# Weight sums of a seven-product FFN stage: GpSimd-issued accumulating transfers in place of VectorE adds, and token sums on VectorE in place of GpSimd

## The reference

```python
D_FF = 2816
def swiglu(h, wi, wo):
    gu = h @ wi
    return (jax.nn.silu(gu[..., :D_FF]) * gu[..., D_FF:]) @ wo

h = rmsnorm(x, ng[4]) * (1.0 + m(7)) + m(6)
x = x + 0.5 * m(8) * rmsnorm(swiglu(h, lw['ffn_wi'][1], lw['ffn_wo'][1]), ng[5])
```

## Time and profile before

| | |
|---|---|
| median of 3 runs | 3124.38 us (3122.71 to 3128.81) |
| the profiled execution's own time | 3123.3 us |
| its span | 3121.5 us |
| PE busy | 2986.2 us, 96% of the span |
| DVE, ACT, POOL busy | 1967.7, 1128.4, 448.3 us |
| TensorE clock granted, mean | 0.974 of full speed |

### The profile page before, as it was taken

The page is one execution under the profiler, slowest core; times in us unless marked ns, Lnnn a source line. Parts: engine busy times, 40 slices in busy tenths (PEclk is TensorE's granted clock), DMA queues, the critical chain, the costliest instruction groups (busy, mean ns, idle before and its releaser), DMA issues.

```text
span 3121.5 us, 63011 instructions
## 1 busy us (share of the span) xinstructions
PE 2986.2 (96%) x26544; PEld 2675.1 (86%) x26544; DVE 1967.7 (63%) x2951; ACT 1128.4 (36%) x1757; POOL 448.3 (14%) x475
## 2 busy tenths in 40 slices
PE   7999999999988899999999999999999889899998
PEld 5999978996777699998789998789877777899986
DVE  3677556556766766765657675652566767688735
ACT  3111245235543441113531112542454435344334
POOL 1000101002323220001100001110022423500100
PEclk8999999999899999999999999999998989999999
DMA  5344344310000234443444333432010004022235
GB/s 225 135 161 153 123 128 162 125 41 27 29 5 13 104 112 158 161 148 111 140 142 161 145 131 130 143 125 84 28 50 7 3 13 149 36 95 82 82 122 168
DMA packets 62655, 324.35 MB, mean 104 GB/s; under 512 B 8753, under 2 KB 12401, under 8 KB 42993
## 3 DMA queue, kind: packets, MB, share of 16 engines
q1 hardware_dynamic: 62448, 321.39, 29.4%
HBM read 318.05 MB, written 3.31 MB: 103 GB/s over the span
## 4 chain that ended last, share of the span: by engine, by line
PE 82%; DVE 8%; DMA 4%; ACT 3%; issue 3%; POOL 0%; SPq 0%; DVEq 0%; ACTq 0%; POOLq 0%
PE PS L2565 39%; PE PS L2677 16%; PE PS L2632 7%; DMA wo<-in_wo 3%; PE PS L2575 3%; PE PS L787 2%; PE PS L1559 2%; DVE wo_lo L3068 2%; PE PS L811 1%; ACT wo_hi L2796 1%; PE PS L1538 1%; PE PS L734 1%; PE PS L1551 1%; PE PS L799 1%; PE PS L1482 1%
## 5 line engine op out<-in xcount | busy, mean ns | idle before, releaser
L2565 PE MATMUL PS<-h_hi,wi_hi 128*128 128x384 f32 (+1 forms) x2784 | 668.3, 310 | 10.5 <-issue 10.5
L2565 PE MATMUL PS<-h_lo,wi_hi 128*128 128x384 f32 (+1 forms) x2784 | 666.1, 309 | 0.0
L2565 PE MATMUL PS<-h_hi,wi_lo 128*128 128x384 f32 (+1 forms) x2784 | 666.0, 309 | 0.0
L2565 PEld LDWEIGHTS PS<-h_hi,wi_hi 128*128 128x128 f32 x2784 | 438.3, 188 | 13.6 <-issue 12.9
L2565 PEld LDWEIGHTS PS<-h_lo,wi_hi 128*128 128x128 f32 x2784 | 438.4, 188 | 0.7
L2565 PEld LDWEIGHTS PS<-h_hi,wi_lo 128*128 128x128 f32 x2784 | 438.2, 188 | 0.7
L3068 DVE TENSOR_TENSOR wo_lo<-wo,wo_hi 128x1024 fp32r<-128x1024 f32 x208 | 256.2, 1232 | 256.4 <-ACT wo_hi L2796 255.3
L2677 PE MATMUL PS<-wo_hi,a_hi 128*128 128x512 f32 x968 | 393.4, 406 | 20.9 <-DVE wo_lo L3068 12.8
L2677 PE MATMUL PS<-wo_hi,a_lo 128*128 128x512 f32 x968 | 378.3, 391 | 0.0
L2677 PE MATMUL PS<-wo_lo,a_hi 128*128 128x512 f32 x968 | 378.1, 391 | 0.0
L2388 DVE SCALAR_TENSOR_TENSOR macc<-wm,csil,macc 128x512 f32<-128x512 f32 x448 | 337.0, 752 | 15.9
(11 more groups left out here) (367 smaller groups left out, 4932.0 us busy)
## 6 DMA issues: line engine op xcount, KB each, us to landing
wi<-in_wi SPq DMA_DIRECT2D x88, 1024.0 KB, 5.0
wo<-in_wo SPq DMA_DIRECT2D x176, 512.0 KB, 3.6
wm<-in_wm SPq DMA_DIRECT2D x36, 2048.0 KB, 7.7
wi<-in_win SPq DMA_DIRECT2D x24, 1024.0 KB, 5.3
wo<-in_wout SPq DMA_DIRECT2D x32, 512.0 KB, 3.6
wq<-in_wq SPq DMA_DIRECT2D x2, 1024.0 KB, 5.0
out_y_sample<-x SPq DMA_DIRECT2D x4, 512.0 KB, 6.7
lvl<-in_lvl SPq DMA_DIRECT2D x2, 896.0 KB, 6.2
```

Source lines behind the costliest of these rows:

```text
L2565: mm = pe.matmul(PSF[0:cols, at:at + GW[g]], st, h[:, k, GA[g]:GA[g] + GW[g]], start=(k == 0 and q == 0), stop=(k == KD - 1 and q == 2))
```

## The change

The seven products are chosen differently, so that each weight sum is the one before it plus one more block of the weights as they lie in HBM. The sums are then made by transfers that POOL issues with an add: `weights_added` adds a 128 x 4 x 128 block (256 KB, rows of 512 bytes) from HBM to a block of the loaded `wi`. There are four a unit: one on the up block (semaphore `s_tu`) and three, one after the other, on the gate block `raw(j, 0, 0)` (`s_ts`). The three change the same block, which is operand 0, then 1, then 2, then 6. So each must wait until the operand before it is cut, and each cut must wait until the transfer has landed. DVE's weight sums are gone. The token sums are made by DVE in place of POOL, two of them before the multiplications of unit 0, two between units 1 and 2. Parts 2, 3, 4 and 6 are accumulated on PSUM banks that already hold parts 0, 1 and 2, after ACT has copied the intermediate value out (`part_copy`). A fast unit uses three banks in place of four, and three DVE additions in place of five; the signs are put right in the final multiplications. The cuts are in another order, `PART_ORDER` = 0, 3, 1, 4, 5, 2, and part 6 of a unit is cut during that unit itself.

```diff
 FAST = {5: 4}
 HT = TOK // 2
 HK = KD // 2
-FAST_BANK = (0, 1, 2, 3, 0, 2, 3)
-CUT_ORDER = (0, 2, 3, 1, 4, 5, 6)
+FAST_BANK = (0, 1, 0, 1, 0, 2, 0)
+SUM_END = (3, 5, 10, 12)
+LOW_END = (6, 7, 13, 14)
+PART_ORDER = (0, 3, 1, 4, 5, 2)
 
...
@@ -359,7 +361,7 @@
 
         def part_source(i, j):
 
-            return (raw(j, 0, 0), raw(j, 0, 0), t3[:], raw(j, 0, 1), raw(j, 1, 0), t4[:], raw(j, 1, 1))[i]
+            return raw(j, *((0, 0), (0, 0), (0, 0), (1, 1), (0, 1), (1, 0), (0, 0))[i])
 
         def part_free(eng, n, u, i):
...
@@ -2462,7 +2464,7 @@
                 if V >= 2:
                     sp.wait_ge(s_wol, V - 1)
                 if b == 0 and n in FAST:
-                    sp.wait_ge(s_pd, 6 * (w0(n) + NF - 1 - FAST[n]) + 2)
+                    sp.wait_ge(s_pd, last_part(n, 2))
                 sp.dma_start(wo[:, V % 2, :, :].rearrange("p k n -> p (k n)"),
                              src[b % 2][OUT_ORDER[SUBS[s]][(b // 2) % OUT_UNITS[SUBS[s]]]]).then_inc(s_wo[V % 2], 16)
@@ -2608,28 +2610,27 @@
                 w, U0 = w0(n) + u - FAST[n], FAST[n]
                 for i in range(7):
                     if i < 6:
-                        pe.wait_ge(s_pl, 6 * w + cut_position(i) + 1)
+                        pe.wait_ge(s_pl, 6 * w + PART_ORDER.index(i) + 1)
                     else:
                         pe.wait_ge(s_wil, u0(n) + u + 1)
-                    if u < U0 + 2:
-                        if i < 4:
-                            pe.wait_ge(s_eb, u0(n) + U0 - (1 if u == U0 and i < 3 else 0))
+                    if i == 0 and u < U0 + 2:
+                        pe.wait_ge(s_eb, u0(n) + u - 1)
                     elif i == 0:
-                        pe.wait_ge(s_pa, 2 * (w - 2) + 2)
-                    elif i < 4:
-                        pe.wait_ge(s_pv, 5 * (w - 2) + (1, 4, 5)[i - 1])
-                    if i == 4:
-                        pe.wait_ge(s_pa, 2 * w + 1)
-                    if i in (5, 6):
-                        pe.wait_ge(s_pv, 5 * w + i - 3)
-                    if u == U0 and i in (1, 2, 3, 6):
-                        pe.wait_ge(s_sl, 4 * list(FAST).index(n) + {3: 1, 1: 2, 2: 3, 6: 4}[i])
-                    dst = PS[:, 4 * (u % 2) + FAST_BANK[i], 0:HT]
+                        pe.wait_ge(s_ea, u0(n) + u - 1)
+                    if i in (1, 5) and u >= U0 + 2:
+                        pe.wait_ge(s_pv, 4 * (w - 2) + (1 if i == 1 else 3))
+                    if i in (2, 3, 4):
+                        pe.wait_ge(s_pa, 4 * w + i - 1)
+                    if i == 6:
+                        pe.wait_ge(s_pv, 4 * w + 2)
+                    if u == U0 and i in (1, 2, 3, 4):
+                        pe.wait_ge(s_sf, LOW_END[-1] * fast_before(n) + LOW_END[(0, 1, 3, 2)[i - 1]])
+                    dst = PS[:, 3 * (u % 2) + FAST_BANK[i], 0:HT]
                     for k in range(HK):
                         a_hi_, a_lo_ = moving(i, k)
                         w_hi_, w_lo_ = part_hi[i][:, k, :], part_lo[i][:, k, :]
                         for q, (st, mv) in enumerate(((w_hi_, a_hi_), (w_hi_, a_lo_), (w_lo_, a_hi_))):
-                            mm = pe.matmul(dst, st, mv, start=(i < 4 and k == 0 and q == 0), stop=True,
+                            mm = pe.matmul(dst, st, mv, start=(i in (0, 1, 5) and k == 0 and q == 0), stop=True,
                                            skip_group_check=True)
                     mm.then_inc(s_pd if i < 6 else s_in, 1)
@@ -2823,15 +2824,15 @@
                 j, w = u % 2, w0(n) + u - FAST[n]
                 act_.wait_ge(s_wi[j], 16 * (u0(n) // 2 + 1) + 8 * (u - j))
                 part_free(act_, n, u, i)
-                if i in (2, 3):
-                    act_.wait_ge(s_ts, 4 * w + (1 if i == 2 else 2))
-                if i in (1, 5):
-                    act_.wait_ge(s_ts, 4 * w + (3 if i == 1 else 4))
+                if i in (1, 2, 6):
+                    act_.wait_ge(s_ts, 16 * (3 * w + {1: 1, 2: 2, 6: 3}[i]))
+                if i == 4:
+                    act_.wait_ge(s_tu, 16 * (w + 1))
                 act_.activation(part_hi[i][:], part_source(i, j), ACT.Copy).then_inc(s_ph if i < 6 else s_wih, 1)
 
             def sum_high(n, m):
 
-                act_.wait_ge(s_sf, 10 * list(FAST).index(n) + (3, 5, 8, 10)[m - 1])
+                act_.wait_ge(s_sf, LOW_END[-1] * fast_before(n) + SUM_END[m - 1])
...
+            def fast_scalar(n):
...
+                    part_copy(n, u, 0, f_p1, 0)
                     if not last:
-                        for i in (0, 2, 3, 1):
+                        part_high(n, u + 1, 0)
+                    part_copy(n, u, 1, f_p5, 1)
+                    part_copy(n, u, 2, f_u2, 0)
+                    part_high(n, u, 6)
                     if last:
...
                     else:
-                        for i in (5, 6):
+                        for i in (3, 1, 4, 5):
                             part_high(n, u + 1, i)
+                    act_.wait_ge(s_pv, 4 * w + 3)
+                    act_.activation(f_p1[:], f_p1[:], ACT.Silu).then_inc(s_pa, 1)
+                    act_.wait_ge(s_in, u0(n) + u + 1)
+                    act_.wait_ge(s_eb, u0(n) + u)
+                    act_.activation(f_s2[:], PS[:, 3 * (u % 2), 0:HT], ACT.Silu).then_inc(s_ea, 1)
+                    if not last:
+                        part_high(n, u + 1, 2)
...
             def cut_wo(n, b):
                 V = V0(n) + b
                 dve.wait_ge(s_woh, V + 1)
+                if b == 1 and n in FAST:
+                    dve.wait_ge(s_pd, last_part(n, 4))
                 dve.tensor_tensor(wo_lo[:, V % 2, :, :], wo[:, V % 2, :, :], wo_hi[:, V % 2, :, :].bitcast(F32),
                                   ALU.subtract).then_inc(s_wol, 1)
 
...
+            def sum_of(n, m):
+
+                a, b = sums[(m - 1) % 2][:], sums[m % 2][:]
...
+                if m == 1:
+                    dve.tensor_tensor(a, hi_(1, 1), hi_(1, 0), ALU.subtract).then_inc(s_sf, 1)
+                    dve.wait_ge(s_sf, base_ + 1)
+                    dve.tensor_tensor(a, a, lo_(1, 1), ALU.add).then_inc(s_sf, 1)
+                    dve.wait_ge(s_sf, base_ + 2)
+                    dve.tensor_tensor(a, a, lo_(1, 0), ALU.subtract).then_inc(s_sf, 1)
+                elif m == 3:
+                    dve.tensor_tensor(a, hi_(0, 0), hi_(1, 0), ALU.subtract).then_inc(s_sf, 1)
+                    dve.wait_ge(s_sf, base_ + 1)
+                    dve.tensor_tensor(a, a, lo_(0, 0), ALU.add).then_inc(s_sf, 1)
+                    dve.wait_ge(s_sf, base_ + 2)
+                    dve.tensor_tensor(a, a, lo_(1, 0), ALU.subtract).then_inc(s_sf, 1)
+                else:
+                    c = m // 2 - 1
+                    dve.scalar_tensor_tensor(out=a, in0=b if m == 2 else a, scalar=-1.0, in1=hi_(0, c), op0=ALU.mult,
+                                             op1=ALU.subtract).then_inc(s_sf, 1)
+                    dve.wait_ge(s_sf, base_ + 1)
+                    dve.tensor_tensor(a, a, lo_(0, c), ALU.subtract).then_inc(s_sf, 1)
+
...
             def fast_vector(n):
...
+                sum_low(n, 1)
+                sum_low(n, 2)
+                sum_of(n, 3)
+                sum_of(n, 4)
+                hidden(n, U0 - 2, 0)
...
+                    bank = lambda b: PS[:, 3 * (u % 2) + b, 0:HT]
                     if not last:
                         part_low(n, u + 1, 0)
+                    dve.wait_ge(s_pd, 6 * w + 4)
+                    dve.wait_ge(s_pa, 4 * w + 3)
+                    dve.tensor_tensor(f_u2[:], f_u2[:], bank(1), ALU.add).then_inc(s_pv, 1)
+                    part_low(n, u, 6)
...
+                        part_low(n, u + 1, 3)
+                        part_low(n, u + 1, 1)
+                    dve.wait_ge(s_pd, 6 * w + 5)
+                    dve.tensor_tensor(f_p5[:], f_p5[:], bank(0), ALU.add).then_inc(s_pv, 1)
...
+                        part_low(n, u + 1, 4)
+                    dve.wait_ge(s_pd, 6 * w + 6)
+                    dve.tensor_tensor(f_p1[:], f_p1[:], bank(2), ALU.add).then_inc(s_pv, 1)
+                    if not last:
+                        part_low(n, u + 1, 5)
+                    dve.wait_ge(s_pa, 4 * w + 4)
+                    dve.wait_ge(s_pv, 4 * w + 1)
+                    dve.scalar_tensor_tensor(out=act[0][:, u, 0:HT], in0=f_u2[:], scalar=-1.0, in1=f_p1[:], op0=ALU.mult,
+                                             op1=ALU.mult).then_inc(s_pv, 1)
+                    dve.wait_ge(s_ea, u0(n) + u + 1)
+                    for dst, cols in ((act[0][:, u, HT:GW[0]], slice(0, GW[0] - HT)), (act[1][:, u, :], slice(GW[0] - HT, HT))):
+                        a = dve.scalar_tensor_tensor(out=dst, in0=f_p5[:, cols], scalar=-1.0, in1=f_s2[:, cols], op0=ALU.mult,
+                                                     op1=ALU.mult)
+                    a.then_inc(s_eb, 1)
+                    if not last:
+                        part_low(n, u + 1, 2)
...
```

(75 more changed lines are left out.)

141 lines of the change are left out of this document (28 added, 113 removed).

## The result

| | before | after |
|---|---|---|
| median | 3126.60 us (3122.71 to 3131.28, 4 runs) | **3256.88 us** (3248.81 to 3266.26, 4 runs) |
| profiled execution, its span | 3123.3, 3121.5 us | 3248.8, 3246.7 us |
| PE busy, share of the span | 2986.2, 96% | 3015.0, 93% |
| DVE, ACT, POOL busy | 1967.7, 1128.4, 448.3 us | 1908.3, 1144.0, 507.3 us |

After over before is 1.0418, with a 95% interval of 1.0398 to 1.0438. The forecast was 3155 us, the range ended at 3235: the sign was right, the size was not.

The account below looks back on a forecast made before the run. TensorE bounded the kernel before, and the ring of transfers would bound the changed fast stage: 3123.3 - 7.6 (start) + 0.3 (end) = 3116.0, plus 17 x 2.29 (ring) = 3155 us; range 3115 to 3235 us.

Parts of the forecast that it names:

- The start: Start of the fast stage, unit 4: TensorE loses 2.0 us in place of 9.63, a gain of 7.6 us.
- The end: End of the fast stage: first output weights loaded after part 2 of unit 21, 1.76 us later, costing +0.3 us.
- The ring: Fast stage: three gate transfers a unit and the cuts between them, each awaiting the last, turn 17 times, adding 17 x 2.29 us.
- the likeliest case: Fast stage: the ring bounds it, landings of 3.5 to 5.9 us; 3155 us, own range 3129 to 3235; chance 0.57.
- R1: Rival, fast stage: the ring fits, L at most 3.24 us, time 3116 us, -0.23%; chance 0.25.
- R2: Rival: the ring almost fits, 3117 to 3129 us, or fits but the start is not won, 3123; chance 0.13.
- P = 3 L + 2.62: Time of one fast unit when the ring exceeds TensorE's 12.33 us: three landings plus two pairs of cuts, 14.62 us.
- L: Gate transfer, from low cut's end to the next high cut's start: taken as 4.0 us, bounds 2.6 and 5.9.
- steps between them: Between a unit's gate transfers: two pairs of high and low cuts, 2 x (0.625 + 0.687) = 2.62 us.
- The load itself is no ring: Fast unit's weight load: starts some 4 us before the unit's end, takes 5.0, before ScalarE reaches it 2.2 us into the next.
- R3: Rival, steady fast stage: GpSimd's transfers slow VectorE's operations from 0.687 to 3.44 us, time 3296 us; chance 0.05.
- The rival price of 2.6 us for a landing: GpSimd's 256 KB gate transfers: about 2.0 us plus bytes at 436 GB/s, 2.6 us; this is R1, chance 0.25.

Follow-up runs that it names:

- experiment 2: The kernel before, with its ten token-sum operations on VectorE in place of GpSimd and the work ahead of the stage reordered to fit: 3117.08 us, ratio 0.9982.
- experiment 3: The changed kernel with the first gate sum of each unit made by VectorE, leaving two gate transfers and the up transfer on GpSimd: 3170.05 us, ratio 1.0147.
- `late_load`: The changed kernel with each unit's 1 MB weight load held back until the first gate transfer of the unit before has landed: 3223.00 us, ratio 1.0316.
- `small_load`: The changed kernel with the plain weight loads of units 6 to 21 cut from 1 MB to 128 KB: 3227.27 us, ratio 1.0322.
- `long_rows`: The changed kernel with each 256 KB weight block laid out in HBM as 128 rows of 2 KB, not 512 of 512 bytes: 3202.48 us, ratio 1.0242.
- `quarter_size`: The changed kernel with each GpSimd transfer adding only 64 KB of the 256 KB, 128 rows of 512 bytes: 3131.55 us, ratio 1.0020.
- `plain_copies`: The changed kernel with GpSimd's four transfers a unit as plain copies without the addition, weight sums left out: 3154.85 us, ratio 1.0085.
- `sync_copies`: The same plain copies as in `plain_copies`, issued by SyncE in its own queue in place of GpSimd's: 3125.15 us, ratio 0.9999 to the kernel before.
- Experiment 5: The run `small_load`: the changed kernel with the weight loads of units 6 to 21 cut from 1 MB to 128 KB, 3227.27 us.
- experiment 4: The run `late_load`: the changed kernel with the 1 MB load held back until the previous unit's first gate transfer landed, 3223.00 us.

## Why the prediction was wrong

*The start: right.* Parts up to part 2 were to start 5.5 us after unit 4; 2721.27 - 2715.82 = 5.45. The token sums on VectorE cost nothing, as said; experiment 2 wins 9.07 us with them alone.

*The end: right without the transfers.* With VectorE's sums the stage takes 224.35 us against 224.3. With the transfers it takes 358.81 us, 1.7 more than 224.3 + 17 x (20.14 - 12.33) = 357.1, and that is a price of the clock that the prediction did not have. TensorE's one piece in the chain of the stage, from the end of unit 20 into unit 21, and the stretch 3058.8 to 3062.3 inside it (length, busy times, granted clock 0.52, DMA share, GB/s):

```profile
3057.79 8.82 PE PS L2633 x48
```

```profile
3058.80:3062.30 3.50, 3.50 (x15) 3.50 (x14) 1.43 (x4) 0.93 (x3) 0.02 (x1) 0.52 0.61 75
```

At full speed it would take 48 x 0.1468 = 7.05 us. It follows a pause of 2.85 us, and for 3.5 us the clock was near the lower of its two levels, 1.2 and 2.4 GHz.

*The ring: right in its form.* That three landings, one after the other, set the time, 17 turns of them, is what the chain shows, and experiment 3 took 5.06 us from a turn with one landing. So the likeliest case came, and R1 (the ring fits) and R2 did not.

*The sizes in P = 3 L + 2.62: wrong. This is the step that failed.* Two terms were too small.

| per turn | predicted | measured | x 17 |
|---|---|---|---|
| three landings | 3 x 4.0 = 12.0 | 3 x 5.36 = 16.07 | 69.1 us |
| steps between them | 2.62 | 4.07 | 24.6 us |
| P | 14.62 | 20.14 | 93.8 us |

(5.36 is the mean landing of the 51 transfers in the 17 turns; the differences are worked out before rounding.) 93.8 us is also 3248.8 - 3155, the whole miss of the profiled execution. That it agrees so well is luck: the 1.7 us at the end and the -2.5 and +0.5 outside the stage nearly cancel. In the prediction's own terms L came to (20.14 - 2.62) / 3 = 5.84 us. That is under its upper bound of 5.9 but above the 5.57 at which the stated range ended.

The steps between first. L was defined from the end of a low cut to the start of the high cut behind it, and then sized by landings alone. Between the low cut and GpSimd's instruction lie 0.28 us, between one landing and the next transfer 0.49, and before each high cut some 0.1. With the two pairs of cuts (0.64 + 0.70 each) this makes 4.0 to 4.1 us wherever GpSimd issues three gate transfers: P minus three mean landings is 4.07 in the changed kernel, 4.08 in `late_load` and `small_load`, 4.04 in `long_rows` and `quarter_size`, 4.12 in `plain_copies`. For no loss the landing itself would have had to be (12.33 - 4.07) / 3 = 2.8 us, not 3.24. The 0.28 and 0.49 belong to GpSimd: in `sync_copies` SP's transfer starts 0.03 us after the low cut and 0.06 us after the landing before it.

Then the landing. I had made 4.0 of a plain copy of 512 KB, 3.6, and a small GpSimd operation, 0.43. Without the load beside it, it is 4.6 to 4.7. The four queue rows above say how much of it the DMA engines work: share times 16 engines times 360 us over the number of transfers gives 34.7, 26.6, 12.7 and 8.8 us of packets per transfer, or 2.2, 1.7, 0.8 and 0.6 us on each of the 16. (69, 72, 72 and 72 transfers fall into the stretch.) So the addition about doubles the packets' time (0.8 to 1.7), a fair guess, and short rows add 0.5 to it, which I only listed and did not price. How the engine spends the time of the addition, the traces do not show.

The rest of the landing is no constant. For the second gate transfer of a unit the packets of the traces give its parts (medians, us):

| | GpSimd's instruction | start to first packet | first to last packet | last packet to landing |
|---|---|---|---|---|
| changed kernel | 1.28 | 1.98 | 2.39 | 0.32 |
| `long_rows` | 0.86 | 1.57 | 2.15 | 0.33 |
| `plain_copies` | 0.75 | 1.46 | 1.51 | 0.35 |
| `quarter_size` | 0.86 | 1.59 | 0.88 | 0.33 |

The first packet comes 0.70 to 0.73 us after the end of GpSimd's instruction in all four. So only about 1.0 us is fixed, and GpSimd's instruction, 0.75 to 1.28 us, is part of every landing. Of what the long rows win in such a transfer, 0.42 us is this instruction and 0.24 the packets.

Last, the collision. First gate transfers average 6.75 us and the other two 4.69 and 4.62, so 2.1 of the 4.1 us by which the landings exceed 12 are this one. I wrote that the load runs beside the transfers and took that for a reason not to go below 4.0; I put no price on it. Experiment 5 shows that the load is the cause, experiment 4 that the order matters. The changed kernel's own turns separate sharply: in all eleven long ones SP issues the load 1.10 to 1.12 us after the first gate transfer's start, in five of the short ones 1.42 to 1.76 us after it, and in the sixth there is no load. The packets show why half a microsecond counts for three. First a long turn (2767.5 to 2773.5 us), then a short one (2749.5 to 2752.0); q0 is the gate transfer, q1 the load:

```profile
q1 hardware_dynamic: 144, 1.05, 49.3%
q0 software_dynamic: 528, 0.26, 36.4%
```

```profile
q0 software_dynamic: 526, 0.26, 90.9%
q1 hardware_dynamic: 31, 0.25, 26.0%
```

528 packets take 6.0 us in one, 526 take 2.5 in the other. When the load's first packet starts, 47 to 78 of the 512 data packets of the gate transfer have started in the eleven long turns, 397 to 442 in the five short ones. Once both are there, the 16 engines start about as many packets of one as of the other, though one's are short and the other's long:

```profile
q1 hardware_dynamic: 96, 0.79, 83.9%
q0 software_dynamic: 107, 0.05, 17.7%
```

(2769.0 to 2771.5 us.) By the shares a packet of the gate transfer takes 0.07 us and one of the load 0.35, so the gate transfer waits most of the time. That fits the other runs. In `late_load` the second gate transfer's packets come behind most of the load's, and it lands after 5.0 us. In `long_rows` there are only 128 data packets to be held back. The up transfer is no part of it: in each long turn it has landed before the load's first packet.

*The load itself is no ring: right.* It took 6.1 us in place of 4.8, but ScalarE waited for GpSimd's transfers, not for it.

*R3, GpSimd and VectorE in each other's way: refuted.* Most cuts do meet GpSimd's transfer instructions: the 74 that overlap one by more than 0.2 us take 687 ns on average, the other 38 take 691. That agrees with the rule of the Trainium skill, "SBUF — State Buffer", section "Who interferes with whom", that would exclude R3.

*The rival price of 2.6 us for a landing: refuted.* It came from the Trainium skill, "DMA: Bandwidth & Descriptors", section "Anatomy of one DMA". The trace disagrees: 3.3 us even for the plain copy from GpSimd, 4.7 with the addition. The page does not say whether its fit is for plain transfers only, as the prediction had it. Section "SWDGE vs HWDGE vs iDMA" of this page in the Trainium skill gives accumulation to GpSimd alone; no run here tried it elsewhere. Its section "Specifications" gives a first byte that comes 0.4 us later by GpSimd's path. The traces agree: on third gate transfers the first packet starts 1.46 us after GpSimd's instruction in `plain_copies` and 1.03 us after SP's in `sync_copies`.

## What to carry to other kernels

A chain of transfers that wait for each other costs its landings and its handoffs: count how many stand one behind the other in a unit, add the handoffs (here half a microsecond for each transfer that GpSimd issued), and compare with the unit, before looking at how idle the DMA engines are. Four VectorE operations of 0.69 us, on an engine with 2.5 us to spare in each unit, were replaced here by transfers of 4.7 us, three of them in a row, on the path. Ask also what other transfer shares the DMA engines at that moment: one cut into many short packets lost 3 us beside one of few long ones. And when a change has two parts, try each alone: the part that helped, moving the token sums off GpSimd, was worth 0.2%, and the other hid it under 4%.
